# Moving the mix-out half, the early products and the constants of a two-block network kernel

## The reference, cut to what matters

```python
# modulation of a layer: 6 x 1024 values for the context and 6 x 1024 for the latent tokens
m = silu(cond) @ w_ada + b_ada            # cond: 1024; w_ada: 1024 x 6144; likewise ada_w_2, two layers each
# layer 0: mixer (RWKV7 scan and chunked SSD), then a gated feed-forward
y  = concatenate([o_rw, y_mb], -1) @ w_out                  # mix-out: 512 + 512 inputs, 1024 outputs
h  = h + m[2] * y
a  = rms_norm(h) * (1 + m[4]) + m[3]
h  = h + m[5] * ((silu(a @ w1) * (a @ w3)) @ w2)            # w1, w3: 1024 x 2816
# o_rw = (group_norm(y_rw) * gn_w + gn_b + bonus) * gate    # ready only after the RWKV7 scan
# y_mb = gated, normed output of the SSD                    # ready long before
```

## Time and profile before

| | us |
|---|---|
| median of three runs | 3348.21 |
| the profiled execution | 3348.48 |
| its span, first to last instruction | 3346.7 |
| TensorE busy | 3127.8 (93%) |
| VectorE busy | 1319.6 (39%) |
| ScalarE busy | 525.2 (16%) |
| mean granted TensorE clock | 0.963 of full |

### The profile page before, as it was taken

One profiled execution on the slowest core, in us unless ns is written; L12 is line 12 of the kernel. 1 busy time (PEld: TensorE's weight loads), 2 busy tenths in 40 slices (PEclk: granted clock), 3 DMA queues, 4 the chain that ended last, 5 costly groups with the idle time before them and its releaser, 6 DMA issues.

```text
span 3346.7 us, 52452 instructions
## 1 busy us (share of the span) xinstructions
PE 3127.8 (93%) x22488; PEld 2078.3 (62%) x22488; DVE 1319.6 (39%) x2980; ACT 525.2 (16%) x1170; POOL 0.2 (0%) x4
## 2 busy tenths in 40 slices
PE   7999899997999997989999999999998879998998
PEld 5454799996344432457865554455557568876887
DVE  1468666665399986721420010001002232112211
ACT  2114222222100000012421100101112120012000
POOL 0000000000000000000000000000000000000000
PEclk8999999998999998999989999999999889999999
DMA  6241001001377784431079999999975113541352
GB/s 247 87 151 50 1 1 39 1 1 52 114 237 233 235 254 146 159 129 51 1 297 346 337 340 345 364 364 355 339 245 164 59 51 126 151 126 51 126 151 63
DMA packets 351450, 551.14 MB, mean 165 GB/s; under 512 B 14496, under 2 KB 292256, under 8 KB 347904
## 3 DMA queue, kind: packets, MB, share of 16 engines
q1 hardware_dynamic: 351232, 547.89, 49.2%
HBM read 546.80 MB, written 1.05 MB: 164 GB/s over the span
## 4 chain that ended last, share of the span: by engine, by line
PE 85%; DVE 10%; ACT 2%; DMA 1%; issue 1%; SPq 0%; DVEq 0%; ACTq 0%
PE bank L653 17%; PE bank L1304 14%; PE bank L914 9%; PE bank L1326 8%; PE bank L1484 7%; PE bank L1095 5%; DVE mix L2030 4%; PE bank L1111 4%; PE bank L617 3%; PE bank L732 3%; PE bank L1138 2%; PE bank L898 1%; PE bank L1249 1%; DMA ring<-in_w_ada 1%; PE bank L1393 1%
## 5 line engine op out<-in xcount | busy, mean ns | idle before, releaser
L653 PE MATMUL bank<-a,ring 128*128 128x256 f32 (+1 forms) x1792 | 454.4, 417 | 22.2 <-ACT a L1581 11.8
L653 PEld LDWEIGHTS bank<-a,ring 128*128 128x128 f32 x1792 | 346.3, 194 | 127.9 <-issue 74.7
L1304 PE MATMUL bank<-ring,arena 128*32 128x352 f32 x5376 | 407.1, 461 | 2.0 <-ACT small L1825 2.0
L2030 DVE SCALAR_TENSOR_TENSOR mix<-arena,csil,mix 128x256 f32<-128x256 f32 x1008 | 405.4, 482 | 0.1
L1095 PE MATMUL bank<-a,ring 128*128 128x512 f32 x704 | 307.8, 597 | 6.8 <-ACT a L1581 6.8
L1304 PEld LDWEIGHTS bank<-ring,arena 128*32 128x32 f32 x5376 | 177.6, 110 | 218.2 <-issue 201.4
L1095 PEld LDWEIGHTS bank<-a,ring 128*128 128x128 f32 x704 | 133.6, 191 | 180.3 <-issue 178.3
L1484 PE MATMUL bank<-arena,ring 128*128 128x256 f32 x1024 | 223.5, 379 | 2.0 <-DVE arena L2684 2.0
L2586 DVE TENSOR_TENSOR arena<-arena,bank 128x352 f32<-128x352 f32 x48 | 25.0, 521 | 501.4 <-ACT arena L1838 501.4
L1585 ACT ACTIVATE arena<-bank 128x256 f32<-128x256 f32 (+1 forms) x303 | 141.8, 473 | 491.1 <-PE bank L914 198.4
L1326 PE MATMUL bank<-ring,arena 128*32 128x256 f32 (+1 forms) x3840 | 218.6, 380 | 0.0
(11 more groups left out here) (409 smaller groups left out, 3325.3 us busy)
## 6 DMA issues: line engine op xcount, KB each, us to landing
ring<-in_moe_w SPq DMA_DIRECT2D x224, 704.0 KB, 8.5
ring<-in_mlp_w SPq DMA_DIRECT2D x64, 1024.0 KB, 5.5
ring<-in_moe_w SPq DMA_DIRECT2D x112, 512.0 KB, 8.5
arena<-in_ada_w SPq DMA_DIRECT2D x96, 512.0 KB, 3.6
arena<-in_w_ada SPq DMA_DIRECT2D x48, 512.0 KB, 3.6
ring<-in_ffn_w SPq DMA_DIRECT2D x22, 1024.0 KB, 7.2
arena<-in_moe_w SPq DMA_DIRECT2D x32, 704.0 KB, 8.9
ring<-in_moe_w SPq DMA_DIRECT2D x48, 384.0 KB, 8.5
```

The source lines that it names most:

```text
L653: i = mm(bank[b][:, 0:n], ws[:, k, t * P:t * P + P], src, start=(k == 0), stop=(k == KT - 1))
L1304: i = mm(b[32 * t:32 * t + 32, 0:PART], ac_[:, k, 32 * g:32 * g + 32], ws[i_][:, PART * t:PART * t + PART], start=(k == 0), stop=(k == KT ...
L2030: ins = V.scalar_tensor_tensor(dst, x, cond, dst, ALU.mult, ALU.add)
```

## The change

`consts` is split: columns 0 to 255 (`ident`, `mean`) are loaded where all were; the rest comes on a semaphore of its own (`more_in`) after slot 2, together with `rows`, `mu_g` and the router. In mix-out the `ym_t` half (k = 4 to 7) of the first five tiles is made before the transposes, into five banks; each tile's other half waits for the heads one by one. The transposes use banks 5 and 6 in turn. `h` is reloaded once the scan's last output is done. Three pairs of the later modulations are made during mix-out, behind residuals 4 to 6. The k = 0 step of every pair is made by ScalarE (`first_parts`) instead of VectorE. The output tiles go to banks 2 to 5, all rows to bank 6, all turned rows to bank 7, and the waits on the columns move. `GROUPS` now has 31 steps, each old step's number being one higher.

```diff
-GROUPS = [3 if j % 4 == 3 else 2 for j in range(FT)] + [3, 3, 3, 3, 3, 3, 3, 2]
+GROUPS = [3] + [3 if j % 4 == 3 else 2 for j in range(FT)] + [3, 3, 3, 3, 2, 2, 2, 2]
+EARLY_PAIRS = ((0,), (1,), (2,), ())
+def pairs_of(g):
+    return [n for n, group in enumerate(GROUP_OF) if group == g]
+EARLY = CO["head"]
+MIX_BANKS = (1, 2, 3, 4, 7)
...
-        ROWS_BANK, TURNED_BANK = (6, 6, 0), (7, 7, 1)
+        ROWS_BANK, TURNED_BANK = 6, 7
...
-            sy.dma_start(consts, w["consts"]).then_inc(consts_in, 16)
+            sy.dma_start(consts[:, 0:EARLY], w["consts"][:, 0:EARLY]).then_inc(consts_in, 16)
...
+                if s < first["mix_out"]:
+                    return -2
...
+                if s == 3:
+                    sy.dma_start(rows, w["rows"]).then_inc(loaded, 16)
+                    sy.dma_start(mug[0:96, :], w["mu_g"]).then_inc(loaded, 16)
+                    sy.dma_start(consts[:, EARLY:NCONST], w["consts"][:, EARLY:NCONST]).then_inc(more_in, 16)
...
                 if s == first["ffn"]:
-                    sy.wait_ge(vec_done, at(VE, "o_rw"))
-                    sy.wait_ge(pe_done, at(PE, ("yr turned", 3)))
+                    sy.wait_ge(pe_done, at(PE, ("y", 15)))
                     for sl, name in ((CTX, "ctxT"), (LAT, "xT")):
...
+                    sy.wait_ge(vec_done, at(VE, "o_rw"))
+                    sy.wait_ge(pe_done, at(PE, ("yr turned", 3)))
                     for chunks_in in range(CHUNKS):
...
-                       GROUP_OF[(chunks_in - CHUNKS) // 2] <= tile_of(s - RING)):
+                       GROUP_OF[(chunks_in - CHUNKS) // 2] - 1 <= tile_of(s - RING)):
...
+            def mix_part(j, ks):
+                sl = first["mix_out"] + j // 2
+                ws = full(sl)
+                for k in ks:
+                    src = mix[:, k, :] if k < 4 else ym_t[:, k - 4, :]
+                    if j == 0 and k < 4:
+                        pe.wait_ge(vec_done, at(VE, "o_rw" if k == 3 else ("o_rw", k)))
+                    i = mm(bank[MIX_BANKS[j % 5]], ws[:, k, j % 2 * P:j % 2 * P + P], src,
+                           start=(k == 4), stop=(k == 3), skip_group_check=True)
...
+            for j in range(5):
+                mix_part(j, (4, 5, 6, 7))
             pe.wait_ge(vec_done, at(VE, "yr norm"))
             for j in range(4):
-                turned(("yr turned", j), lambda m: yt[:, m, j * P:j * P + P], 1 + j)
-            pe.wait_ge(vec_done, at(VE, "o_rw"))
-            product("mix out", first["mix_out"], 4, mix, slice(0, T), [6, 7],
-                    lambda j: pe.wait_ge(vec_done, at(VE, ("mix res", j))), more=ym_t,
-                    then=lambda j: square_in(1, slice(0, T), j))
+                if j >= 2:
+                    pe.wait_ge(act_done, at(AC, ("gn", j - 2)))
+                turned(("yr turned", j), lambda m: yt[:, m, j * P:j * P + P], 5 + j % 2)
+            for j in range(KT):
+                if j >= 5:
+                    pe.wait_ge(vec_done, at(VE, ("mix res", j - 5)))
+                    mix_part(j, (4, 5, 6, 7))
+                mix_part(j, (0, 1, 2, 3))
+                if j:
+                    square_in(1, slice(0, T), j - 1)
+            square_in(1, slice(0, T), KT - 1)
...
-                    if j and i_ == 0:
-                        sum_up(j - 1)
-                    if j >= 2 and i_ == 0:
-                        turn_later(j - 2)
+                    if i_ == 0:
+                        sum_up(j)
+                        if j:
+                            turn_later(j - 1)
...
-                elif n == 2:
-                    pe.wait_ge(vec_done, at(VE, ("later", 1)))
                 for k in range(FT):
-                    i = mm(bank[4 + n % 4], ws[:, k, :], G[:, k, :], start=(k == 0), stop=(k == FT - 1))
+                    i = mm(bank[2 + n % 4], ws[:, k, :], G[:, k, :], start=(k == 0), stop=(k == FT - 1))
...
-            pe.wait_ge(vec_done, at(VE, ("later", 2)))
             pe.wait_ge(vec_done, at(VE, ("var", 2)))
...
             pe.wait_ge(act_done, at(AC, ("q1", 7)))
+            pe.wait_ge(vec_done, at(VE, ("later", 2)))
...
+            def first_parts(ns):
+                for n in ns:
+                    ac.wait_ge(chunk_full[2 * n % CHUNKS], 16 * (2 * n // CHUNKS + 1))
+                    if n >= SUMS:
+                        ac.wait_ge(pe_done, at(PE, ("summed", (n - SUMS) // 4)))
+                    for s in range(2):
+                        copy(("first part", n, s), sums[n % SUMS][:, s, :], chunk[2 * n % CHUNKS][:, 0, :],
+                             csil[:, LATER[n // ADA][0], 0, s:s + 1])
+            for k in range(KT):
+                ac.wait_ge(vec_done, at(VE, ("mix res", k)))
+                square(1, slice(0, T), k)
+                if k >= 4:
+                    first_parts(EARLY_PAIRS[k - 4])
             norm(1, slice(0, T))
+            first_parts(pairs_of(1))
...
-                later_rows_out(j - 1)
+                later_rows_out(j)
+                first_parts(pairs_of(j + 2))
...
-                        for s in range(2):
+                        for s in range(2 if k else 0):
...
-                            if k == 0:
-                                ins = V.tensor_scalar(dst, x, cond, None, ALU.mult)
+                            if k == 1:
+                                ve.wait_ge(act_done, at(AC, ("first part", n, s)))
...
+                if j >= 4:
+                    products_by_partition(EARLY_PAIRS[j - 4])
```

More of the change, by code:

```diff
@@ L395, in build @@
         chunk = [cut(arena, FT * T + 1024 * i, 4, 256) for i in range(CHUNKS)]
-        sums = [cut(mix_t, 512 * i, 2, 256) for i in range(SUMS)]
+        sums = [cut(mix_t, 512 * ((i + 4) % SUMS), 2, 256) for i in range(SUMS)]
         later_rows = arena[:, 15360:15872]
-        ROWS_BANK, TURNED_BANK = (6, 6, 0), (7, 7, 1)
+        ROWS_BANK, TURNED_BANK = 6, 7
         q1 = cut(arena, 0, KT, TL)
@@ L459, in build @@
         SQUARES = {st: aT if st in (0, 1, 2, 4) else mix for st in range(14)}
-        SUM_BANK = {st: {2: 2, 4: 4, 13: 3}.get(st, 0) for st in range(14)}
+        SUM_BANK = {st: {4: 4, 13: 3}.get(st, 0) for st in range(14)}
         block = ctx.enter_context(nc.Block())
@@ L637, in normed, with product @@
                 pe.wait_ge(act_done, at(AC, ("norm", st, k, 1)))
-            def product(name, s0, n_slots, rhs, sl, banks, before, of=None, then=None, more=None):
+            def product(name, s0, n_slots, rhs, sl, banks, before, of=None, then=None):
                 n = sl.stop - sl.start
@@ L651, in product @@
                                 normed(of, k)
-                            src = rhs[:, k, sl] if more is None or k < 4 else more[:, k - 4, sl]
-                            i = mm(bank[b][:, 0:n], ws[:, k, t * P:t * P + P], src,
+                            i = mm(bank[b][:, 0:n], ws[:, k, t * P:t * P + P], rhs[:, k, sl],
                                    start=(k == 0), stop=(k == KT - 1))
@@ L751, in _ @@
             i.then_inc(pe_done, did(PE, "gram"))
+            pe.wait_ge(more_in, 16)
             pe.wait_ge(vec_done, at(VE, "a_tok"))
@@ L1065, in sum_up @@
                     of, m = q // 6, q % 6
-                    if of == 1 and m == 0:
-                        pe.wait_ge(act_done, at(AC, ("later rows", 0)))
+                    if of and m == 0:
+                        pe.wait_ge(act_done, at(AC, ("later rows", of - 1)))
                     for t in range(4):
@@ L1070, in sum_up @@
                         pe.wait_ge(vec_done, at(VE, ("chunk", 2 * n + 1)))
-                        i = mm(bank[ROWS_BANK[of]][32 * t:32 * t + 32, :], const("one", 64)[:, 31 - m:63 - m],
+                        i = mm(bank[ROWS_BANK][32 * t:32 * t + 32, :], const("one", 64)[:, 31 - m:63 - m],
                                sums[n % SUMS].rearrange("p s n -> p (s n)"), start=(m == 0), stop=(m == 5),
@@ L1080, in turn_later @@
                     pe.wait_ge(act_done, at(AC, ("later rows", of)))
-                    if of == 1:
-                        pe.wait_ge(vec_done, at(VE, ("later", 0)))
-                    turned(("later", of), lambda m: later_rows[:, m * P:m * P + P], TURNED_BANK[of])
+                    if of:
+                        pe.wait_ge(vec_done, at(VE, ("later", of - 1)))
+                    turned(("later", of), lambda m: later_rows[:, m * P:m * P + P], TURNED_BANK)
             for j in range(FT):
@@ L1753, in later_rows_out @@
                     ac.wait_ge(pe_done, at(PE, ("summed", 6 * of + 5)))
-                    copy(("later rows", of), later_rows, bank[ROWS_BANK[of]])
+                    copy(("later rows", of), later_rows, bank[ROWS_BANK])
             for j in range(FT):
@@ L2012, in scales, with products_by_partition @@
                                                ).then_inc(vec_done, did(VE, ("gs", g)))
-            def products_by_partition(g):
-                for n in (n for n, group in enumerate(GROUP_OF) if group == g):
-                    if n >= SUMS:
```

(9 more changed lines are left out.)

51 lines of the change are left out of this document (27 added, 24 removed).

## The result

The changed kernel's median is 3301.43 us over four runs (3293.41, 3297.04, 3305.83, 3306.97), the kernel before had 3348.45 beside it (3347.99 to 3352.48): a ratio of 0.9859, interval 0.9835 to 0.9883, some 47 us faster. The profiled execution took 3293.41 us, span 3291.6; that of before 3348.48 and 3346.7. The prediction named 3294.4 for the profiled execution and 3294 for the median. The median missed its figure by 7.4 us; the profiled execution, the fastest of the four, came within 1.0. Since both figures were summed from the traces, trace against trace is the fair test of the single terms, and the scatter of the runs (13.6 us here) is larger than most of them.

What follows compares the result with a forecast made beforehand. TensorE bounds the kernel, busy 93% of the span, its waits the quick gain. 5.1 + 18.0 - 1.4 + 6.3 + 22.7 + 3.4 = 54.1 us, so 3294.4 us for the profiled execution, 3294 median; range 3287 to 3303.

Steps and rivals of the forecast that it cites:

- 1. Start: Kernel start: first weights no longer queue behind most of the constants, 5.1 us won (bounds 4 to 5.4).
- 2. Mix-out: Mix-out: halves of five tiles fill TensorE's gap, 19.5 us less 1.5 for a clock fall, 18.0 won (bounds 14.5 to 20).
- 3. Feed-forward tiles: Feed-forward tiles: quad 11 is summed here, one sum and four transposes more, 1.4 us given back; VectorE stays hidden.
- 4. The last gated product: Before the first output tile: TensorE's 7.30 us idle for this product falls to 1.0, 6.3 us won (bounds 2 to 6.5).
- 5. Output tiles: Output tiles: 194.7 us become 172.0 as the wait for the second layer's columns goes, 22.7 won (bounds 19 to 33).
- stall for pair 60: Behind output tile 2: pair 60 waits for quad 13's sum, delaying a square; TensorE idles 7.7 us, plus 3.1 of half clock.
- residual 0 at about 35, wanted at 39: Output tiles: VectorE makes three pairs (16.6 us), three more (33.2), then residual 0 at about 35, before its need at 39.
- (c): Output tiles: the knot at pair 60 dissolves, 10.8 us less, 3283; chance 0.05.
- 6. The seam: Output tiles to attention: rows copied earlier and projections no longer wait for the last columns, 3.4 us won (bounds 1.5 to 5).
- (a): VectorE's pairs: each waits for both of ScalarE's copies, 6.44 us a pair, giving 3314; chance 0.12.
- (b): Between 48 and 805 us: something hangs on SyncE's order and the early gain is lost, 3299; chance 0.06.
- (d): Feed-forward and output tiles: ScalarE's copies and VectorE's products disturb one another in SBUF, slower, 3374 at p = 7.6; chance 0.03.

Runs made afterwards that it cites:

- the kernel with the late half: Changed kernel with all sixteen matmuls of every mix-out tile run after the transposes' wait, none made ahead: 3315.76 us, ratio 0.9893.
- the last experiment: Changed kernel with quad 13 summed behind output tile 1 instead of 2: 3281.31 us, ratio 0.9792.
- the last experiment but one: Changed kernel with both the early pairs and the new banks with their column waits undone: 3317.61 us, ratio 0.99.
- the banks experiment: Changed kernel with the old output, rows and turned banks and their two waits on the columns, early pairs kept: 3298.18 us, ratio 0.9846.

## Why the prediction was right, step by step

The forecast, its order of terms and the shape of the new trace hold. That the sum came within 1.0 us of the profiled execution is partly luck: the terms' misses and the parts without a term add up to some 8 us by size and cancel for the most part, and the execution was the fastest of four. Against the two medians (47.0 and 58.6 us faster than the kernel beside them) the forecast of 54.1 lies between. The terms in turn:

**1. Start.** Predicted 5.1 us, the time by which the first weights come earlier; the last weight tile came at 30.20 instead of 35.11, 4.9. On top came about 1.5 by the scan's end, most of it (1.3) in the L728 matmuls, where the clock fell later in this trace. The prediction had no term for that, and none was due: the unaltered repeat took 9.45 there, as before (9.58). It is a lucky part of the agreement.

**2. Mix-out.** Predicted 18.0 of a possible 19.5; it was 19.4. The step that was off is the 1.5 us set aside for a fall of the clock: it did not fall in the stretch where TensorE was busy 4.13 of 5 us. The prediction had weighed that fall by the busy share of two windows. The stretch of L728 shows that this share alone does not decide it: there the clock fell with TensorE busy all the time. The fall and its cost do show where the gap is long, in the kernel with the late half (13.42 us idle, then 0.50 from 813 to 819). The Trainium skill, "TensorE: Matmul & The Clock Gate", section HAM oscillation, tells of matmul bursts that are shorter than the waits between them, and of an array at half rate after each wait. The long gap agrees with it. The short ones are no case of it: here the waits of 0.20 to 0.43 us are shorter than the work between them (1.04 to 4.56 us). The early pairs fit: VectorE's 14 products took 5.63 us beside a period of 7.73, behind a wait of 1.17 for ScalarE (5.54 and 1.13 predicted):

```profile
849.74 5.63 DVE L2079 SCALAR_TENSOR_TENSOR mix<-arena,csil,mix 128x256 f32<-128x256 f32 x14 [1.17 <-ACT mix L1618]
```

What was wrong was their place in the reasoning, not their cost (step 5).

**3. Feed-forward tiles.** Predicted 1.4 given back, measured 0.9. VectorE is again hidden there. The kernel without early pairs has these tiles 1.6 us shorter, so the term itself was sound. The difference lies at the start, where the first products run at half clock: by their durations less 0.429 us a product, that costs 2.6 us before (80 products in 36.89) and 1.8 after (48 in 22.38), an estimate.

**4. The last gated product.** Predicted 6.3 us of gain, measured 5.2: an idle time of 2.06 and not 1.0. The trace after names what stands ahead of it. VectorE had to wait for a chunk, and now ScalarE stands between chunk and VectorE: the chain goes from the transfer (1171.24, 10.12) over ScalarE's copy at 1181.38 to VectorE.

**5. Output tiles.** Predicted 172.0 us, measured 174.6, the mis-sized term. The stall for pair 60 was right in place and size: 8.15 us, the norm sum at 2.08 for 0.86 and the tile at 20.32 for 18.88, together 10.8 as predicted (8.15 of idle time and 2.7 of half clock, forecast as 7.7 and 3.1). Short by 2.6 were 1.25 us behind tile 1, four norm sums that took 1.06 to 1.12 us and not 0.86, and 0.5 in the first two tiles. The prediction had named a second stall among these tiles as a sign of being wrong; the 1.25 us are one, if a small one. The step that failed here is "residual 0 at about 35, wanted at 39". The two kinds of row that explain it, ScalarE's and VectorE's timeline:

```profile
1209.04 0.91 ACT L1618 ACTIVATE mix<-arena,csil 128x256 f32<-128x256 f32 x2 [14.59 <-DMA arena<-in_ada_w]
...
1226.55 0.91 ACT L1618 ACTIVATE mix<-arena,csil 128x256 f32<-128x256 f32 x2 [10.07 <-DMA arena<-in_ada_w]
...
1255.70 0.91 ACT L1618 ACTIVATE mix<-arena,csil 128x256 f32<-128x256 f32 x2 [19.87 <-PE bank L1106]
```

```profile
1209.65 16.71 DVE L2079 SCALAR_TENSOR_TENSOR mix<-arena,csil,mix 128x256 f32<-128x256 f32 x42 [4.15 <-ACT mix L1618]
1227.16 5.63 DVE L2079 SCALAR_TENSOR_TENSOR mix<-arena,csil,mix 128x256 f32<-128x256 f32 x14 [0.79 <-ACT mix L1618]
...
1256.31 5.63 DVE L2079 SCALAR_TENSOR_TENSOR mix<-arena,csil,mix 128x256 f32<-128x256 f32 x14 [10.40 <-ACT mix L1618]
```

The prediction had VectorE run freely through six pairs, with residual 0 at about 35 us behind the first output tile's start. It waits 4.15 and 0.79 us for chunks; the chain shows their transfers 10.95 and 8.84 us long. Residual 0 comes at 1232.79, 39.0 us behind the tile's start, and ends 0.8 later. In this stretch 1408 KB slots and 512 KB chunks share the queue. That the slots are what delays the chunks was not tried. The third row of each is the known stall: the name in VectorE's bracket is ScalarE, but ScalarE had itself waited 19.87 us for the sum of quad 13, and moving that sum by one tile, in the last experiment, took all of it away. That gain, 12.2 us in the output tiles, is what rival (c) describes, with 10.8 estimated for it, and the 1.25 us behind tile 1, which went too; it needed an edit of its own.

The prediction also credited the lost 17.1 us to the pairs and the banks together. The size was right (the last experiment but one has 15.91 and 2.75 of half clock back), the reading incomplete: the experiments show that either would have done alone, so that undoing one shows about 0 (pairs) or 3 us (banks), while undoing both costs 23 us more than undoing the pairs alone and 19 more than undoing the banks alone.

**6. The seam.** Predicted 3.4, measured 3.65; the banks experiment puts 2.5 of it down to the wait on the columns, which that kernel has back.

**Rivals.** (a) and (b) are refuted by their experiments, and the stall of 8.15 us decides against (c). Against (d), that copies and products disturb one another, stand the durations (minimum/median/maximum ns, first and last start), first the products before, then copies and products in the changed kernel:

```profile
L2030 DVE SCALAR_TENSOR_TENSOR mix<-arena,csil,mix x1008: 468/481/495, 901.8 to 1407.9; 128x256 f32<-128x256 f32 x168
...
L1618 ACT ACTIVATE mix<-arena,csil x144: 491/494/511, 841.4 to 1339.4; 128x256 f32<-128x256 f32 x144
L2079 DVE SCALAR_TENSOR_TENSOR mix<-arena,csil,mix x1008: 466/476/486, 842.0 to 1345.9; 128x256 f32<-128x256 f32 x168
```

VectorE's products lasted 481 ns in the median before and 476 beside the copies: no disturbance. The Trainium skill, "SBUF — State Buffer", section Who interferes with whom, gives ScalarE ports of its own, and this trace agrees.

## What to carry to other kernels

Work that is ready early and sits behind a wait is worth more than its idle time: here 17 us of products moved into a gap, together with the waits head by head, removed 13.4 us of idle time and the half-rate stretch behind it, 19.4 in all. When two edits both remove one wait, undoing one shows nothing of it; undo both before either is called useless or useful. And when a stall survives a change, follow the name in the bracket one step further: the engine named was itself waiting, for a sum that could be issued one tile earlier, and this one line gave 12.2 us in the output tiles.

## What the runs showed of the hardware that was not expected

TensorE kept its 2.4 GHz through gaps of 0.2 to 0.4 us, busy 4.13 us of a 5 us stretch, and was at 1.2 GHz behind the gap of 13.4 us. It also fell to 1.2 GHz with no gap at all: in the 64 matmuls of L728 (128x16), TensorE was busy in every one of the 10 us from 67 to 77, and the clock went from 1.00 to 0.50 between 73 and 74. All ten traces show a clock of 1.00 at the start of these matmuls and 0.50 before their end. What brings the fall is not shown. Its moment moves from run to run: the same 64 matmuls took 8.28 and 9.45 us in two traces of one kernel, and up to 11.24 in the others, with nearly the same work ahead of them. So up to 3 us of a difference between two traces can come from here, whatever was edited.

The kernel before, unaltered, spread over 4.5 us in four runs beside the changed kernel and over 20 us in eleven on another chip. So terms of a few us had to be read from traces, and medians compared within one chip.
